# T blocks of the feed-forward weights: from VectorE's subtractions to accumulating DMAs

## The reference

```python
def _swiglu(x, w_gate, w_up, w_down):
    return (jax.nn.silu(x @ w_gate) * (x @ w_up)) @ w_down
...
        x = _layer_norm(alpha * x + 0.5 * _swiglu(x, ffn1_w_gate[i], ffn1_w_up[i], ffn1_w_down[i]),
                        ln_gain[i, 0], ln_bias[i, 0])
```

## Time and profile before

| what | value |
|---|---|
| median of 3 runs | 1333.76 us (1333.35 to 1335.18) |
| the profiled execution, its own time | 1333.44 us |
| its span, first to last instruction | 1331.7 us |
| mean granted TensorE clock | 0.998 |
| PE, PEld busy | 1318.7, 1131.3 us |
| VectorE busy | 1092.0 us |
| ScalarE busy | 774.3 us |
| GpSimd busy | 123.3 us |
| data moved | 241.98 MB, 182 GB/s on average |

### The profile page before, as it was taken

How to read it: one execution, slowest core, us unless ns; L and a number is a source line. 1 busy time by engine, 2 the same in 40 slices (tenths; PEclk the granted TensorE clock), 3 DMA queues, 4 the chain that set the end, 5 groups by cost and what they waited for, 6 DMA issues and landing times.

```text
span 1331.7 us, 19263 instructions
## 1 busy us (share of the span) xinstructions
PE 1318.7 (99%) x7332; PEld 1131.3 (85%) x7333; DVE 1092.0 (82%) x1348; ACT 774.3 (58%) x1057; POOL 123.3 (9%) x235
## 2 busy tenths in 40 slices
PE   9999999999999999999999999999999999999997
PEld 6988999998888889988888888888889988888886
DVE  6877776777998885687998888988886988999886
ACT  6674555555655644586665565656656854565561
POOL 5430000000000111184000000000000001000000
PEclk9999999999999999999999999999999999999999
DMA  9425766666557276504764638467165535855721
GB/s 327 155 81 174 244 197 189 187 203 243 172 175 252 70 246 206 190 17 163 264 210 145 214 126 292 156 217 255 61 196 186 173 93 156 306 173 173 253 70 57
DMA packets 164625, 241.98 MB, mean 182 GB/s; under 512 B 7041, under 2 KB 122002, under 8 KB 164546
## 3 DMA queue, kind: packets, MB, share of 16 engines
q1 hardware_dynamic: 158960, 226.52, 51.1%
q0 software_dynamic: 5296, 13.29, 3.2%
q10 hardware_dynamic: 290, 1.11, 0.2%
HBM read 238.24 MB, written 1.07 MB: 180 GB/s over the span
## 4 chain that ended last, share of the span: by engine, by line
PE 91%; DVE 6%; issue 2%; DMA 0%; ACT 0%; POOL 0%; SPq 0%; DVEq 0%
PE ps L894 18%; PE ps L896 18%; PE ps L895 18%; PE ps L716 7%; PE ps L717 6%; PE ps L718 6%; PE ps L917 2%; PE ps L918 2%; PE ps L924 2%; DVE wlo L640 2%; DVE wlo L677 2%; PE ps L1845 1%; PE ps L3129 1%; PE ps L1077 1%; PE ps L1051 1%
## 5 line engine op out<-in xcount | busy, mean ns | idle before, releaser
L640 DVE TENSOR_TENSOR wlo<-raw,whi 128x1024 fp32r<-128x1024 f32 x262 | 310.6, 1221 | 34.3 <-ACT whi L630 33.7
L630 ACT ACTIVATE whi<-raw 128x1024 fp32r<-128x1024 f32 x262 | 264.8, 1053 | 60.0 <-PE ps L896 41.7
L677 DVE TENSOR_TENSOR wlo<-arena,whi 128x2048 fp32r<-128x2048 f32 x84 | 191.7, 2290 | 54.2 <-ACT whi L666 54.2
L666 ACT ACTIVATE whi<-arena 128x2048 fp32r<-128x2048 f32 x84 | 161.0, 1916 | 107.6 <-PE ps L896 107.6
L894 PE MATMUL ps<-whi,ahi 128*128 128x512 f32 x536 | 212.2, 396 | 0.0
L896 PE MATMUL ps<-wlo,ahi 128*128 128x512 f32 x536 | 209.1, 390 | 0.0
L895 PE MATMUL ps<-whi,alo 128*128 128x512 f32 x536 | 208.7, 389 | 0.0
L716 PE MATMUL ps<-ahi,whi 128*128 128x256 f32 x624 | 177.9, 285 | 0.0
L717 PE MATMUL ps<-alo,whi 128*128 128x256 f32 x624 | 177.3, 284 | 0.0
L718 PE MATMUL ps<-ahi,wlo 128*128 128x256 f32 x624 | 177.2, 284 | 0.0
L716 PEld LDWEIGHTS ps<-ahi,whi 128*128 128x128 f32 x624 | 120.4, 193 | 0.9 <-issue 0.3
(11 more groups left out here) (470 smaller groups left out, 2393.0 us busy)
## 6 DMA issues: line engine op xcount, KB each, us to landing
raw<-ffn_w_down SPq DMA_DIRECT2D x88, 512.0 KB, 4.6
arena<-ffn_w_gate SPq DMA_DIRECT2D x24, 1024.0 KB, 5.1
arena<-ffn_w_up SPq DMA_DIRECT2D x24, 1024.0 KB, 5.6
raw<-w_up SPq DMA_DIRECT2D x44, 512.0 KB, 4.4
raw<-ffn_w_gate SPq DMA_DIRECT2D x40, 512.0 KB, 4.2
raw<-ffn_w_up SPq DMA_DIRECT2D x40, 512.0 KB, 4.9
raw<-w_down SPq DMA_DIRECT2D x22, 512.0 KB, 4.2
raw<-w_in SPq DMA_DIRECT2D x16, 512.0 KB, 5.5
```

The costliest lines, as they stand in the source:

```text
L630: act.activation(split_half(w_slots(slot)[0], mode), raw_half(h), ACT.Copy).then_inc(hi_ready, 1)
L640: dve.tensor_tensor(lo, raw_half(h), hi.bitcast(F32), ALU.subtract).then_inc(lo_ready, 1)
L666: act.activation(hi, src, ACT.Copy).then_inc(hi_ready, 2)
L677: dve.tensor_tensor(lo, src, hi.bitcast(F32), ALU.subtract).then_inc(lo_ready, 2)
```

## The change

VectorE's T subtractions go, except T3 of the first double step of each stage. In their place ScalarE writes -r11 into n1 and -r22 into n2 (activation Copy with scale -1), and GpSimd issues DMAs that add one SBUF buffer onto another (accum_op add): n1 += r12 gives T1; r12 += n2 gives -T3; n2 += n1 gives -T2; r21 += n2 gives T4. For the two negative ones the sums of activations that they are multiplied by change sign (s_sum 1 and 2). The semaphore t_landed counts the DMAs, sixteen for each, and unit_copied takes in ScalarE's two negations beside the three copies that snap_ready counted. Each accumulate waits for the one before it, T4's also for b21's wlo. In the first double step of a stage -T3 stays a subtraction on VectorE, and the chain of DMAs is T1, T2, T4. That makes 44 DMAs of 1 MB and 24 negations in place of 44 subtractions. PE's and SP's instructions are the same.

```diff
--- before.py
+++ after.py
...
         block_landed = {"r11": (b1_landed, 32), "r12": (b1_landed, 32), "r21": (b21_landed, 16), "r22": (b22_landed, 16)}
-        t_ready = sem("t_ready")
+        t_landed = sem("t_landed")
...
         s_lo_ready = sem("s_lo_ready")
-        snap_ready = sem("snap_ready")
+        unit_copied = sem("unit_copied")
...
         act_chain = sem("act_chain")
...
             if name[0] == "t":
-                act.wait_ge(t_ready, 4 * g.d + int(name[1]))
+                if (g.d, name) in t_at:
+                    act.wait_ge(t_landed, t_count(g.d, name))
+                else:
+                    act.wait_ge(sums_ready, 2 * ffn_index(n) + 2)
...
                 act.wait_ge(landed_at, each * (g.d + 1))
...
-        def dve_t(dve, g, i):
-
-            r11, r12, r21, r22, n1, n2 = (flat_blocks[name] for name in ("r11", "r12", "r21", "r22", "n1", "n2"))
-            if i == 1:
-                dve.wait_ge(b1_landed, 32 * (g.d + 1))
-                dst, a, b = n1, r12, r11
-            elif i == 2:
-                dve.wait_ge(b22_landed, 16 * (g.d + 1))
-                dve.wait_ge(t_ready, 4 * g.d + 1)
-                dst, a, b = n2, r22, n1
-            elif i == 3:
-                dst, a, b = r12, r22, r12
+        def double_before(n, g):
+            return next((x for x in reversed(groups[n]) if x.double and x.d == g.d - 1), None)
+
+        t_at = {}
+        for n in groups:
+            for g in groups[n]:
+                if g.double:
+                    for name in ("t1", "t2", "t4") if double_before(n, g) is None else ("t1", "t3", "t2", "t4"):
+                        t_at[g.d, name] = 16 * (len(t_at) + 1)
+
+        def t_count(d, name):
+            return t_at[d, name]
+
+        def dve_first_t3(dve, n, g):
+            dve.wait_ge(t_landed, t_count(g.d, "t1"))
+            dve.wait_ge(b22_landed, 16 * (g.d + 1))
+            dve.tensor_tensor(flat_blocks["r12"], flat_blocks["r12"], flat_blocks["r22"],
+                              ALU.subtract).then_inc(sums_ready, 1)
+
+        def act_negate_first(act, n, g):
+
+            before = double_before(n, g)
+            act.wait_ge(b1_landed, 32 * (g.d + 1))
+            if before is None:
+                act.wait_ge(sums_ready, 2 * ffn_index(n) + 1)
             else:
-                dve.wait_ge(b21_landed, 16 * (g.d + 1))
-                dve.wait_ge(t_ready, 4 * g.d + 2)
-                dst, a, b = r21, r21, n2
-            dve.tensor_tensor(dst, a, b, ALU.subtract).then_inc(t_ready, 1)
+                act.wait_ge(lo_ready, before.at["t2"] + 2)
+            act.activation(flat_blocks["n1"], flat_blocks["r11"], ACT.Copy, scale=-1.0).then_inc(unit_copied, 1)
+
+        def act_negate_second(act, n, g):
+
+            before = double_before(n, g)
+            act.wait_ge(b22_landed, 16 * (g.d + 1))
+            if before is None:
+                act.wait_ge(s_lo_ready, ffn_index(n) + 1)
+            else:
+                act.wait_ge(lo_ready, before.at["t2"] + 2)
+                act.wait_ge(t_landed, t_count(before.d, "t4"))
+            act.activation(flat_blocks["n2"], flat_blocks["r22"], ACT.Copy, scale=-1.0).then_inc(unit_copied, 1)
+
+        def pool_sums(pool, n):
+
+            r12, r21, n1, n2 = (flat_blocks[name] for name in ("r12", "r21", "n1", "n2"))
+
+            def add(dst, src):
+                pool.dma_start(dst, src, accum_op=ALU.add).then_inc(t_landed, 16)
+
+            for g in groups[n]:
+                if not g.double:
+                    continue
+                pool.wait_ge(unit_copied, 5 * g.d + 1)
+                add(n1, r12)
+                pool.wait_ge(unit_copied, 5 * g.d + 2)
+                pool.wait_ge(t_landed, t_count(g.d, "t1"))
+                if (g.d, "t3") in t_at:
+                    add(r12, n2)
+                    pool.wait_ge(t_landed, t_count(g.d, "t3"))
+                add(n2, n1)
+                pool.wait_ge(lo_ready, g.at["b21"] + 2)
+                pool.wait_ge(t_landed, t_count(g.d, "t2"))
+                add(r21, n2)
...
         def act_split_next(act, n, j, s):
...
                 turn(own, range(NT))
-                pe.wait_ge(snap_ready, 3 * d + 1)
+                pe.wait_ge(unit_copied, 5 * d + 3)
                 product("t2", block_sum(2), z, False, True)
                 down_step(g, parts[i - 1].steps[0], (ghi, glo))
-                pe.wait_ge(snap_ready, 3 * d + 3)
+                pe.wait_ge(unit_copied, 5 * d + 5)
...
                 pe.wait_ge(c_ready, 2 * d + 2)
...
                 act_block(act, n, c + 3)
+                if i == 1:
+                    act_negate_second(act, n, parts[2])
...
                 if before.double:
...
                 act.wait_ge(half_done, g.at["b11"] + 2)
-                act.activation(v1, z, ACT.Copy).then_inc(snap_ready, 1)
+                act.activation(v1, z, ACT.Copy).then_inc(unit_copied, 1)
                 act_block(act, n, c + 4)
                 act.wait_ge(half_done, g.at["t1"] + 2)
-                act.activation(v5, ps[:, 1, :], ACT.Copy).then_inc(snap_ready, 1)
+                act.activation(v5, ps[:, 1, :], ACT.Copy).then_inc(unit_copied, 1)
...
                 act.wait_ge(half_done, g.at["t2"] + 2)
-                act.activation(v_u2, z, ACT.Copy).then_inc(snap_ready, 1)
+                act.activation(v_u2, z, ACT.Copy).then_inc(unit_copied, 1)
...
                 act_block(act, n, c + 7)
+                following = parts[i + 2] if i + 2 < final else None
                 act_block(act, n, c + 8)
+                if following is not None:
+                    act_negate_first(act, n, following)
                 act_block(act, n, c + 9)
+                if following is not None:
+                    act_negate_second(act, n, following)
...
                 act_block(act, n, c + 10)
...
             silu(0, 1)
-            act.wait_ge(sums_ready, f + 1)
+            act_negate_first(act, n, parts[2])
...
                            ACT.Copy).then_inc(x_copied, 1)
...
             def single(i):
...
                 g, c = parts[i], place_of(n, parts[i].at["k0"])
-                before, following = parts[i - 1], parts[i + 1]
-                if following.double and before.double:
-                    dve_t(dve, following, 1)
+                before = parts[i - 1]
...
                     dve.wait_ge(x_copied, 5 * f + 5)
...
                 product(i, 0)
-                if following.double:
-                    dve.wait_ge(s_lo_ready, f + 1)
-                    dve_t(dve, following, 2)
...
                     dve_block(dve, n, c + 4)
-                    if following.double:
-                        dve_t(dve, following, 3)
                     dve_block(dve, n, c + 5)
-                    if following.double:
-                        dve_t(dve, following, 4)
...
                     dve_block(dve, n, c + 4)
-                    if following.double:
-                        dve_t(dve, following, 3)
+                    dve_first_t3(dve, n, parts[2])
...
             def double(i):
...
                 dve_block(dve, n, c + 3)
-                dve.wait_ge(snap_ready, 3 * d + 1)
+                dve.wait_ge(unit_copied, 5 * d + 3)
...
                 turned((0, 1), turns + parts[i - 1].steps[0] + 1)
-                if i == 2:
-                    dve_t(dve, g, 4)
...
                 dve.wait_ge(half_done, g.at["t3"] + 2)
-                dve.wait_ge(snap_ready, 3 * d + 3)
+                dve.wait_ge(unit_copied, 5 * d + 5)
...
                 dve.wait_ge(half_done, g.at["b22"] + 2)
...
             dve.wait_ge(x_copied, 5 * f + 4)
-            dve.tensor_tensor(s_sum[:, 2, :], x11, x21, ALU.subtract)
+            dve.tensor_tensor(s_sum[:, 2, :], x21, x11, ALU.subtract)
             link(dve, dve_chain, "dve", dve.tensor_tensor(s_sum[:, 0, :], x21, x22, ALU.add))
-            link(dve, dve_chain, "dve", dve.tensor_tensor(s_sum[:, 1, :], s_sum[:, 0, :], x11, ALU.subtract))
-            dve.tensor_tensor(s_sum[:, 3, :], x12, s_sum[:, 1, :], ALU.subtract).then_inc(sums_ready, 1)
+            link(dve, dve_chain, "dve", dve.tensor_tensor(s_sum[:, 1, :], x11, s_sum[:, 0, :], ALU.subtract))
+            dve.tensor_tensor(s_sum[:, 3, :], x12, s_sum[:, 1, :], ALU.add).then_inc(sums_ready, 1)
             product(0, 1)
             dve_block(dve, n, 3)
-            dve.wait_ge(sums_ready, f + 1)
-            dve_t(dve, parts[2], 1)
...
             for i in range(1, final):
...
                 if parts[i].double:
...
             pool_load_gb(pool, 3)
+            pool_sums(pool, 3)
...
                 pool_rstd(pool, 3, a)
...
                 if p > 4:
...
                     pool_load_gb(pool, p)
+                    pool_sums(pool, (6, 7)[p - 5])
...
                     pool.dma_start(r_gain, io["hgrn_norm_gain_2"].rearrange("a d -> d a")).then_inc(r_gain_landed, 16)
...
             pool_load_gb(pool, 8)
+            pool_sums(pool, 10)
...
```

## The result

| what | before | after |
|---|---|---|
| median of 4 runs each | 1333.55 us (1331.78 to 1335.18) | 1375.45 us (1373.89 to 1380.08) |
| ratio | | 1.0323, 95% interval 1.0306 to 1.0339 |
| the profiled execution, its own time and span | 1333.44, 1331.7 us | 1380.08, 1378.3 us |
| mean granted TensorE clock | 0.998 | 0.986 |

The forecast was 1349.5 us with a range up to 1378: the sign and the place were right, and the size was not. The table speaks of +42 us by the medians.

A forecast was written before the change was run, and what follows sets the result against it. TensorE, busy 99%, was taken to bound the kernel, VectorE's 82% not. Late T2 at +17.6 us and the t1 gain of -1.5 sum to +16.1 on 1333.44, giving 1349.5 us; range 1331.5 to 1378, the forecast's own 1337 to 1375.

The forecast's parts named there:

- What bounds the kernel: Four feed-forward stages: TensorE busy throughout, VectorE's 82% no bound; only TensorE's waits for VectorE can be won, 2.0 us at most.
- What goes, -1.5 us: First double steps of layers 6, 7 and 10: t1 comes sooner without T1 and T2 on VectorE, 0.5 us each.
- ScalarE's negations at nothing: Two scaled copies in each of 12 double steps, 46 us of ScalarE, were claimed to delay nothing on TensorE.
- Rival 3: ScalarE's negations become the wait if r22 lands late: 4.4 us at g1, eight times, 35 us, 1368 us; chance 0.03.
- One accumulate, 7.1 us alone: One 1 MB accumulating DMA: 1.9 us plus 2.1 MB at 400 GB/s, 7.1 us, between bounds 4.8 and 11.6.
- How late T2 comes: Eight later double steps: T3 lands at 388.7, T2 at 395.8, 2.2 us late each, +17.6 us in all.
- the budget of 28.2 us: Later double steps: time for T1, T3 and T2, from first negation at 365.4 to T2 wanted by 393.6; 9.4 each.
- The price of a wait: Later double steps: T2's lateness was multiplied by eight, with no term for TensorE's clock after a wait.
- What stands behind the waiting copy: ScalarE's queue: copies of TensorE's products stand behind its wait for each T; no size was given.
- The first double steps, free up to A = 8.2: First double step of each stage: late T2 costs nothing while one accumulate, A, takes up to 8.2 us (layer 3: 9.0).
- No change: Rival 1: accumulates run at copy rate or share with little loss, average A under 9.4; 1332.0 us, chance 0.40.
- The slowest one: Rival 2: an accumulate takes 11.6 us even alone; 6.6 us in eight steps, 2.8 in four, some 1398 us; chance 0.10.

## Why the prediction was right in direction and wrong in size

**What bounds the kernel: right.** The list of waits gave 2.0 us as the most that could be won. Plain copies, half accumulates and light loads came out 1.3, 2.4 and 1.7 us under before, and each interval takes in 2.0; in their traces the gain at t1 is 1.5.

**What goes, -1.5 us: right.** The three gaps shrank by 1.3 us together, and layer 3's t1 came 0.2 earlier.

**ScalarE's negations at nothing: nearly right.** 24 negations of 1.91 us cost 1.3 us by the medians (0.3 to 2.8 by the interval), 1.1 of it seen at t1. In the steady state they cost nothing, as priced: the first ran at 362.07, the second at 365.77, the Silu behind them at 367.58, and PE's transposes waited for none of them. Rival 3 is out.

**One accumulate, 7.1 us alone: right.** 6.8 at the least, a median of 7.4 where the loads were light. The form that it was taken from, 2.1 MB at 400 GB/s behind 1.9 us, fits what half accumulates and copies measured.

**How late T2 comes: the first step that failed, by its size.** The sum booked 2.2 us for each of the eight later steps, and PE's t2 starts 3.0 to 4.7 us late, 3.8 on average: 12.8 of the 26 us by which the median lies over the forecast (30.6 in the profiled execution). T2 was put at 7.1 us and took 7.2 on average. Two other terms were small slips with a large effect, since the lateness is the difference of 30.4 and 28.2. **T1 and T3 together, put at 9.3 MB at 400 GB/s or 23.3 us, took 23.9 to 25.2, on average 24.4.** It was not that the other steps had more traffic than the earlier trace rows: the weight queue moves 5.0 to 5.2 MB between T1's issue and T2's landing in each of the eight. Its lines for the first of them, 364.27 to 395.35, and for the latest one, layer 7's, 891.90 to 924.13:

```profile
q1 hardware_dynamic: 3150, 5.11, 48.9%
q1 hardware_dynamic: 3148, 5.10, 45.5%
```

With 4.9 MB of loads and 4.2 for T1 and T3, 24.4 us are an estimate of 375 GB/s on average and not 400; the handing over from one accumulate to the next is in it (377.17 to 377.70 in the chain above), for which the sum had no term. **And the budget of 28.2 us was 27.8 from T1's issue on:** in layer 3 PE would have begun t2 at 396.63, T2 landed 4.5 us before PE's start, and T1 was issued at 364.27, 0.3 behind the end of the negation. In four steps, layer 3's first among them, the load of r11 for the next double step is issued while T2 is under way (392.73 and 920.08), and T2 takes 7.2 to 7.8 us there against 6.8 to 6.9 in the others.

**The price of a wait: the second step that failed. It was put at nothing, and without a word.** The prediction multiplied the lateness by eight and stopped there. The clock falls with most waits of 3 to 5 us, and the matmuls after it start 0.43 us apart in place of 0.23 until it is back: 13.2 us in the kernel after, the largest single thing missing from the sum, and 1.4 us for each us of waiting, all told, in the kernels with repeated copies. The windows of the stages show 1.00 throughout, and PE never waits that long there, so that the fall could not be read from the rows chosen; what the lower level costs stands in the trace of before, in the window at 55.3 us.

**What stands behind the waiting copy: seen, and not priced.** The prediction says that "the copies of PE's products stand behind that wait", and gives it no number. It is the wait for glo: 3.8 us in the kernel after, 2.7 in the one with T3 on VectorE.

**The first double steps, free up to A = 8.2: wrong by a little.** T2 takes 7.3 to 8.0 us there, below the bound, and yet t2 starts 0.6, 0.2 and 0.8 us late in layers 6, 7 and 10. The sum let T2 start with the end of its negation and left T1 out. In layer 6 the negation ends at 670.74, but T1, issued at 661.09, takes 10.0 us beside the loads and lands at 671.11; then only is T2 issued:

```profile
671.66 0.88 POOL L727 DMA_DIRECT2D arena<-arena  x1 [9.68 <-DMA arena<-arena]
```

And glo, further down, is late too; its slack was never looked up. A step is not free because its first reader is in time; each reader in the queue behind has to be asked.

**The rivals.** No change (0.40) would have needed an average A of 9.4, or 9.3 by the budget as measured, and got 10.3 to 10.8 until T2's landing. Plain copies, half accumulates and light loads all came out as that rival says, with averages of 7.3 to 8.3: the point from which it decides lies between. The slowest one (0.10, 1398) had the wrong price, 11.6 alone, and a slip in its sum: by the prediction's own slacks of 8.2 and 9.0 the four first steps cost 12.8 us and not 11.2. With 42 us the measured time lies a little nearer to it than to the forecast, but the cause is the forecast's late T2 and what follows from it.

**Outside of the accumulates** the weight loads got slower too, which I had not booked and which cost nothing here: a down block lands in 6.5 us in place of 4.6, and a gate or up block of 0.5 MB in 8.3 or 9.7 where it was 4.2 or 4.9.

## What to carry to other kernels

Price a wait of PE by its length and what its clock loses after it, and price a late instruction by everything queued behind it on its in-order engine. Count an accumulating DMA as twice its bytes against the DMA engines' time in the stretch where it runs, and do not book the engines' best rate over a whole chain: where budget and chain are both near 30 us, 4% more on the chain is over half of the 2.2 us that were booked. Where a chain of them has a budget, one link can break it: here the same change with one of four sums left on VectorE lost 4 us in place of 42.

## What the runs showed of the hardware

- An accumulating DMA of 1 MB from SBUF to SBUF takes the DMA engines twice as long as a copy (49.3% against 25.2% of the same 41 us) and lands in 6.8 us at the least, 7.4 where little runs beside it, 9.5 (up to 13.6) beside weight loads. A plain copy at the same places: 4.4 at the least, median 5.9, at most 9.6. Half an accumulate: 4.4, 4.9 and 10.9. Whether it is the second read or the addition that doubles it, no run here separates.
- Its issue takes GpSimd 0.87 us, that of a plain copy 0.53.
- With the accumulates the two queues ask for 49.3% and 48.6% of the engines' time in these 41 us, 98% together, and the loads of the weight queue land in up to twice the time (a block of 0.5 MB in 9.7 us for 4.9).
- PE's granted clock fell to the 1.2 GHz level (0.50) with each of eight waits listed at 4.6 us, and with four of eight equally long ones of 2.6 us, with no accumulating DMA in the kernel. With accumulates it fell with six of eight: with one of 2.8 us, not with two of 3.0 and 3.1. Matmuls of 512 columns then start 0.43 us apart in place of 0.23.
